# A gated order of first transfers and a respread mixer in an eight-core hybrid decoder step

## The reference

```
h = rmsnorm(x);  [u|v|p|q|gates] = h @ w_in          # 512|512|256|256|3*1024 columns
A: vh = layernorm(gelu(v)); a = gelu(u) * (tril(W_s[g]) @ vh + b_s[g])   per chunk of 128
B: mean over the trailing 2/4/8/16 rows of p, minus p, then a grouped linear layer
C: 4-head attention of q into 256 memory tokens
   prompt: k, v = rmsnorm(mem) @ w_kv;  sample: k, v are given per sequence
x += (sig(gA)*(a@Wa) + sig(gB)*(b@Wb) + sig(gC)*(c@Wc)) @ w_o
x += relu(rmsnorm(x) @ w_up)^2 @ w_down;  y = rmsnorm(x)
```

## Time and profile before

| | |
|---|---|
| median of 3 runs | 1034.17 us (1028.15 to 1060.0) |
| the profiled execution | 1025.52 us |
| its span, slowest core (core 1) | 1023.8 us |
| spans of all cores | 1016.1 to 1023.8 us |
| mean granted PE clock of core 1 | 0.969 |
| PE busy | 931.6 us (91%) |
| DVE, ACT, POOL busy | 384.8, 294.8, 274.1 us |
| first PE instruction | 35.85 us |

### The profile page before, as it was taken

One profiled execution on the slowest core, in us unless ns is written; L12 is line 12 of the kernel. 1 busy time (PEld: TensorE's weight loads), 2 busy tenths in 40 slices (PEclk: granted clock), 3 DMA queues, 4 the chain that ended last, 5 costly groups with the idle time before them and its releaser, 6 DMA issues.

```text
span 1023.8 us, 15629 instructions; the slowest of 8 cores (1016.1 to 1023.8 us)
## 1 busy us (share of the span) xinstructions
PE 931.6 (91%) x5312; PEld 481.7 (47%) x5312; DVE 384.8 (38%) x640; ACT 294.8 (29%) x528; POOL 274.1 (27%) x280
## 2 busy tenths in 40 slices
PE   0485878887999999999999999999999999999996
PEld 0253444444555555555555554455444554455442
DVE  0356455544223223223553124412343224421476
ACT  0144535252222222222555320033001320033332
POOL 1114113223433433434333320032101230023243
PEclk9987898897999999999999999999999999999998
DMA  9856630449102222221505022040404004040034
GB/s 143 214 151 143 125 118 1 83 82 239 28 16 41 42 42 42 42 42 65 162 1 104 1 44 41 11 72 1 83 1 83 1 11 72 1 83 2 21 152 178
DMA packets 17081, 71.26 MB, mean 70 GB/s; under 512 B 2141, under 2 KB 3164, under 8 KB 13164
## 3 DMA queue, kind: packets, MB, share of 16 engines
q0 software_dynamic: 5472, 35.65, 20.6%
q1 hardware_dynamic: 11532, 34.61, 10.3%
HBM read 95.80 MB, written 10.22 MB: 104 GB/s over the span
## 4 chain that ended last, share of the span: by engine, by line
PE 89%; DMA 4%; DVE 2%; issue 2%; POOL 1%; SPq 1%; ACT 1%; DVEq 0%; POOLq 0%; ACTq 0%
PE bank L338 87%; DMA X<-x 3%; PE bank L341 2%; SPq L153 1%; POOL X L347 1%; DMA cvo<-fA 1%; DVE X L356 1%; ACT fA L344 0%; ACT CR L344 0%; DVE fA L356 0%; POOL stats L347 0%; DVE hT L362 0%; DVEq L125 0%; DVE X L353 0%; ACT X L344 0%
## 5 line engine op out<-in xcount | busy, mean ns | idle before, releaser
L338 PE MATMUL bank<-hT,slot 128*128 128x436 bf16 (+3 forms) x2480 | 471.0, 350 | 0.0
L338 PEld LDWEIGHTS bank<-hT,slot 128*128 128x128 bf16 x2480 | 241.8, 99 | 218.0 <-issue 8.9
L338 PE MATMUL bank<-slot,CR 128*128 128x512 bf16 (+1 forms) x1376 | 298.5, 378 | 0.0
L344 ACT ACTIVATE fA<-bank 128x436 f32<-128x436 f32 (+3 forms) x223 | 120.2, 542 | 373.8 <-PE bank L338 359.8
L338 PEld LDWEIGHTS bank<-slot,CR 128*128 128x128 bf16 x1376 | 134.0, 98 | 157.0
L356 DVE SCALAR_TENSOR_TENSOR X<-bank,stats,X 128x512 f32<-128x512 f32 x136 | 102.1, 751 | 119.4 <-PE bank L338 119.4
L344 ACT ACTIVATE fW<-bank 128x436 f32<-128x436 f32 (+2 forms) x106 | 56.2, 533 | 174.7 <-PE bank L338 173.7
L347 POOL TENSOR_TENSOR CR<-fA 128x436 bf16<-128x436 f32 (+1 forms) x69 | 66.5, 964 | 108.7 <-ACT fA L344 104.3
L347 DVE TENSOR_TENSOR fA<-bank,fA 128x436 f32<-128x436 f32 (+1 forms) x77 | 43.1, 605 | 106.7 <-PE bank L338 106.6
L347 DVE TENSOR_TENSOR CR<-fA 128x436 bf16<-128x436 f32 (+1 forms) x51 | 31.2, 612 | 116.6 <-ACT fA L344 116.6
L347 POOL TENSOR_TENSOR stats<-stats,cstt 128x1 f32<-128x1 f32 (+3 forms) x30 | 35.5, 1185 | 139.5 <-DVE stats L353 115.5
(11 more groups left out here) (87 smaller groups left out, 496.0 us busy)
## 6 DMA issues: line engine op xcount, KB each, us to landing
slot<-wpk POOLq DMA_DIRECT2D x30, 1024.0 KB, 12.3
X<-x SPq DMA_DIRECT2D x34, 512.0 KB, 11.8
y<-hT SPq DMA_DIRECT2D x17, 512.0 KB, 2.7
CR<-ck POOLq DMA_DIRECT2D x4, 512.0 KB, 8.0
CR<-cv POOLq DMA_DIRECT2D x4, 512.0 KB, 11.0
gb<-gvec SPq DMA_DIRECT2D x3, 512.0 KB, 15.3
CR<-mem SPq DMA_DIRECT2D x2, 512.0 KB, 8.9
fW<-gbv SPq DMA_DIRECT2D x4, 256.0 KB, 14.0
```

The costliest lines, as they stand in the source:

```text
L338: s.op("pe", lambda e: e.matmul(out, lhsT=lhsT, rhs=rhs, start=start, stop=stop), R_, W_)
L344: s.op("act", lambda e: e.activation(out=out, in_=in_, func=func, **kw), R_, W_)
```

## The change

It does these things:

- **Transfers at the start.** `dma` and `load_next` take an `after` list of buffers whose last transfer is waited for. The load of v waits for x tile 0, pq for x tile 2, u for v, kv for pq. The window tables (`bnd`) are loaded ahead of the memory, and x tiles 4 to 6 ahead of the spatial-gate setup.
- **Block 0.** `P` and `WIN(0)` come ahead of the memory norms, squares of tiles 4 to 7 are laid between the gelus of `U`, `KV` comes ahead of `MIX`. `KV`'s evictions move from ACT to DVE, its bf16 copies from POOL to ACT.
- **Blocks 1 to 3.** The order inside a block becomes Q, V, S, P with `vout`, WIN, AV, U, MIX. Squares and multiplications of the next block's tiles are laid into a block ahead.
- **Sample tile.** Its norm, transpose and `Q(4)` stay in block 1, at its end. `V(16)`, `P(16)`, `WIN(4)`, and u and the gate (now `U4` and `MIX4`, one wide call each) go to block 3.
- **Sample attention.** `SA2` is cut in two (`SA2b` is its second half), and the steps are spread between P, WIN, AV and U.
- **Stores.** The `cvo` and `pool` outputs use tiles of the `xst` or `xnA` ring (`tS`) in place of `fA` and `fW`; the 16 small `pool_s` transfers are one. The first merge product (`WPO(0)`) is made ahead of the last `MIX`.

```diff
-    def dma(self, queue, pairs, reads=(), writes=(), owner=None):
+    def dma(self, queue, pairs, reads=(), writes=(), owner=None, after=()):
...
+        for b in self._flat(after):
+            op.deps.append(b.last_w)
...
-        load_next("v")
-        load_next("pq")
-        load_next("u")
+        x_b = [norm_src[t][1] for t in BT[0]]
+        load_next("v", after=[x_b[0]])
...
+            if i == 2:
+                load_next("pq", after=[x_b[2]])
...
+        load_next("u", after=[slot_b[0]])
+        s.dma("sp", [(bnd[:, B_CUR:B_SC], cb[:, B_CUR:B_SC])], writes=[bnd_b], owner=bnd_b)
         gm, gm_b = mem_loads()
-        load_next("kv")
+        load_x([4, 5, 6])
         setup_loads()
-        load_x([4, 5, 6])
...
         vfin()
+        load_next("kv", after=[slot_b[1]])
...
+        def tS(t):
+            if t == 16:
+                xn, xnb = ring("xn", xnA, xnA_b)
+                return xn.bitcast(F32), xnb
+            xt, xb = ring("xst", xst, xst_b)
+            return xt[:, 0:512], xb
...
-                    s.dma("sp", [(pool_s[b, 7:15, :], po[b * 8:(b + 1) * 8, 0:256]) for b in range(16)], reads=[po_b], owner=po_b)
+                    s.dma("sp", [(pool_s[:, 7:15, :], po[:, 0:256])], reads=[po_b], owner=po_b)
...
-                CP("act", f[:, 0:256], bk[:, 0:256], [bk_b], [f_b])
-                CP("pool", v_p[:, t, :], f[:, 0:256], [f_b], [vp_b])
+                CP("dve", f[:, 0:256], bk[:, 0:256], [bk_b], [f_b])
+                CP("act", v_p[:, t, :], f[:, 0:256], [f_b], [vp_b])
...
             S(j, 0)
             S(j, 1)
             if j >= 2:
-                SA1(2 * (j - 2))
-                SA1(2 * (j - 2) + 1)
...
+                SA1(g0)
+                SA1(g1)
+            for i in range(4):
+                P(BT[j][i])
+                vout(i)
+            if j == 3:
+                flush()
+                P(16)
+                vout(4)
...
+                    if g == 0:
+                        norm_sq(n16, 16)
+                        norm_b(*n16)
+                        N(16)
+                        load_x([12])
...
+                T(16)
+                Q(4)
...
+            if j == 3:
+                WPO(0)
...
+            if j == 3:
+                MIX4(*u4)
```

More of the change, by code:

```diff
@@ L387, in build_program, with load_next @@
         ld = {"n": 0}
-        def load_next(expect=None):
+        def load_next(expect=None, after=()):
             if ld["n"] >= len(order):
@@ L410, in build_program, with norm_new, norm_sq, norm_b @@
         xn_of = {}
-        def norm_a(ts):
[L413 to L423, removed]
+        def norm_new(n):
+            c = statcols(2 * n)
+            return [c, n, s.buf("st%d" % c), 0]
+        def norm_sq(nb, t):
+            c, n, sb_, i = nb
+            nb[3] += 1
+            xt, xb = norm_src[t]
+            xn, xnb = ring("xn", xnA, xnA_b)
+            ACT(xn, xt, AF.Square, [xb], [xnb, sb_], accum_out=stats[:, c + i:c + i + 1])
+            xn_of[t] = (xn, xnb, c + n + i, sb_)
+        def norm_a(ts):
+            nb = norm_new(len(ts))
+            for t in ts:
+                norm_sq(nb, t)
+            return nb
+        def norm_b(c, n, sb_, _):
             TS("dve", stats[:, c:c + n], stats[:, c:c + n], 1.0 / 1024, EPS, ALU.mult, ALU.add, [sb_], [sb_])
@@ new lines, in MIX, with U4 @@
+            tm, tm_b = tA()
+            STT(tm[:].rearrange("p (t i) -> p t i", i=128), bk[:, :].rearrange("p (t i) -> p t i", i=128), gvcol[:, g:g + 1],
+                CC[0][:, g:g + 1, :].broadcast_to([128, 4, 128]), ALU.mult, ALU.add, [bk_b, CC_b[0], cst_b], [tm_b])
+            TT("pool", apre[:, g, c0:c1], tm[:], ug[:], ALU.mult, [tm_b, ug_b], [apre_b[g][j]])
+        def U4():
+            w, wb = W("u", 8)
+            bk, bk_b = pb()
+            for g in range(4):
+                for k in range(8):
+                    MM(bk[:, g * 128:(g + 1) * 128], w[:, k, g * 128:(g + 1) * 128], hT[:, k, 2048:2176], k == 0, k == 7, [hT_b[16], wb], [bk_b])
+            ug, ug_b = tW()
+            ACT(ug[:], bk[:, :], AF.Gelu_apprx_tanh, [bk_b], [ug_b])
+            return ug, ug_b
@@ new lines, in MIX4 @@
+        def MIX4(ug, ug_b):
+            bk, bk_b = pb()
+            for g in range(4):
+                MM(bk[:, g * 128:(g + 1) * 128], vhs[:, g * 128:(g + 1) * 128], wsT[1][:, g, :], True, True, [vhs_b, wsT_b[1]], [bk_b])
+            tm, tm_b = tW()
+            for g in range(4):
+                STT(tm[:, g * 128:(g + 1) * 128], bk[:, g * 128:(g + 1) * 128], gvcol[:, g:g + 1], CC[1][:, g, :], ALU.mult, ALU.add,
+                    [bk_b, CC_b[1], cst_b], [tm_b])
+            TT("pool", apre[:, :, 2048:2176], tm[:].rearrange("p (g i) -> p g i", g=4), ug[:].rearrange("p (g i) -> p g i", g=4), ALU.mult,
+               [tm_b, ug_b], [apre_b[g][4] for g in range(4)])
```

201 lines of the change are left out of this document (108 added, 93 removed).

## The result

| | before | changed |
|---|---|---|
| first comparison, median of 4 runs each | 1034.3 us | 996.2 us (987.8 to 996.4) |
| ratio, 95% interval | | 0.9631 [0.9556, 0.9706] |
| second comparison, beside three of its variants | 1035.8 us, 11 runs | 986.7 us, 6 runs |
| ratio, 95% interval | | 0.9532 [0.95, 0.9563] |

The account below looks back on a forecast made before the run. Before 246 us PE stands waiting for x tiles and in the blocks, at a lowered clock; behind it PE is busy. Gains 20 + 5 + 20 = 45 us: 1025.5 - 45 = 980.5, plus 6.5 towards the median, 987 us (969 to 1009).

Parts of the forecast that it names:

- Start to the first V: From the start to the first `V` product: it comes at 27 us instead of 43, within 23 to 31.
- the slow end: Start: x tiles beside weight loads move at some 50 KB a microsecond, so tile 2 lands at 21 us; 20 taken.
- To the scores: First `V` to block 0's scores: they start at 70 us instead of 90, 20 us gained, bounds 14 and 26.
- the ends 64 and 71: Start of block 0's scores: 64 us at 150 KB a microsecond beside weight loads, 71 at some 50.
- The end of block 0: Scores to end of block 0: tile 16's transpose and 5.8 us wait leave; 5 us gained (3 to 6).
- Blocks 1 to 3: 104 to 246 us: 14 us net from waits and 6 from the clock, together 20 us gained (8 to 27).
- The sum of 24.7: Blocks 1 to 3 and first merge tile: PE waits of 11.0 + 6.2 + 2.7 + 2.3 + 2.5 us, expected to go.
- the chain that I had on ACT: Blocks 1 to 3: table load, eight exponentials, four evictions of `P` and a correction, 8 to 10 us, make `WIN` wait 6.
- The price of nothing for POOL behind the gains: Block 3: POOL's `cvo` multiplications wait for their gain, with merge loads queued behind; priced at nothing, up to 5 us if uncovered.
- Rival 1: The start stays bound by bytes: scores at 80 us, 10 us earlier instead of 20; 35 us gained, 997 us; chance 0.20.
- Rival 2: Waits of blocks 1 to 3 only change names, no clock returned: 5 us there, 30 in all, 1002 us; chance 0.10.
- Rival 4: Slower: a clock of 0.81 carries into the merge and behind, 180 us less 45, about 1165 us; chance 0.04.

Follow-up runs that it names:

- e6: Changed kernel with the gates undone: v, pq and u issued at once, kv at its old place, block 0's new order kept; 997.3 us, ratio 0.9628.
- e2: Changed kernel with the start and block 0 of the kernel before, blocks 1 to 3 as changed; 1006.7 us, ratio 0.9809.
- e8: Changed kernel with two of the four `V` products put ahead of `Q` in block 1; 984.6 us, ratio 0.9579.
- e9: Changed kernel with the sample attention's spreading undone: `SA2b` directly behind its `SA2`, both `SA3` together; 993.1 us, ratio 0.9654.
- e10: Changed kernel with the `cvo` rows multiplied in their `fA` tiles again and the store sent earlier; 988.3 us, ratio 0.9607.
- e3: Changed kernel with the four `P` products put ahead of `S` in blocks 1 to 3; 987.4 us, ratio 0.9627.
- e11: e8 with, besides, the last `V` product of each block (in block 3 the last two) behind the scores; 996.8 us, ratio 0.9701.

## Why the prediction was right, and where its steps were off

| term | forecast | measured (means of cores) |
|---|---|---|
| first `V` | 43 to 27 | 41.2 to 25.7 |
| gain at the scores | 20 (14 to 26) | 22.0 |
| to the end of block 0 | 5 (3 to 6) | 15.2 - 13.6 = 1.6 |
| blocks 1 to 3 and the first merge tile | 20 (8 to 27) | (131.2 - 117.6) + (786.5 - 781.3) = 18.8 |
| sum | 45 | 42.4 |

The last but one term is the length from block 1 to the merge and from there to the end.

**Start to the first V**: right in sum, by errors that cancel. Tile 0 landed at 7.8 us (1.96 + 5.8), not 5.5; the 3.2 us of the earlier trace rows are those of a tile alone, and here the gain and the next tiles of its own queue travel with it, which is the likely cause. So v came at 8.39 + 14.5 = 22.9, not 19 to 20. But the tiles went faster than the slow end: tile 2 landed at 15.5 us, not 20, and tile 1's transpose came at 19.2, not 23. What the forecast left out is tile 3. The transpose of tile 2 stands behind the statistics of tile 3, which landed at 23.1, and PE waits 5.8 us there; v had landed 3.9 us before the first `V`. The chain that ended last names that tile too:

```profile
4.12 18.93 DMA X<-x
```

On seven cores it is tile 3, on core 0 it is v, by 0.8 us. e6 shows that the gates cause the gain. The loads of pq, u and kv were issued 3.3 to 5.8 us behind the landing that they wait for, since a power that isn't ready stands in front of each in POOL's order; PE lost nothing by it, but for at most 1.4 us for pq on core 0.

**To the scores**: between the ends 64 and 71, at 65.8. No one waits for u or kv, as forecast. The gate tables were not "just ahead": the setup product waits 1.96 us for `wpb` on core 3 and up to 4.2 on others. Both ends came from a rate beside weight loads. The rule of "DMA: Bandwidth & Descriptors" in the Trainium skill, section "Queues, rings and completion order", would have given 71; the trace lies between it and the row of 150 KB a microsecond. While tile 3 travelled beside v, from 15.5 to 23 us, the two queues moved 0.81 and 0.79 MB, as by that rule.

**The end of block 0** is a step that failed: 1.6 us, not 5, below the range of 3 to 6. The wait of 5.8 us for tile 16 left, but I let nothing take its place. Two waits did (PE, 67 to 81 us):

```profile
PE bank L341 <- DVE hT L365: 2.5, 1, 2.5
PE bank L341 <- DVE fA L359: 2.2, 3, 1.5
```

The last copies into `hT`, which the transpose of tile 16 had covered, now stand directly ahead of `Q`, and `S` waits for banks that `MIX` still holds. e2 tells the two apart: with the old block 0, where `KV` lies between `MIX` and `S`, it has the 2.5 us for `hT` and none for `MIX`'s banks, and wins 3.8 us here. So the rest goes to the new block 0. e8 removes the wait for `hT`: 10.9 us instead of 13.6.

**Blocks 1 to 3**: right in sum, with the gain from waits too high and that from the clock too low, and with the wrong waits named, so in part by luck. The waits: 14 net forecast; idle time fell by 21.9 - 14.7 = 7.2, and by 2.6 in the first merge tile, 9.8. The sum of 24.7 that was to go held the 5.0 us around `S`, for which no step of mine takes the cause away; they have become the 5.6 for `ACT CR` and the 1.8 for `DVE CR`. Of the new waits, `WIN` was priced at 6 us (3.2, 1.5, 1.5) and has 1.8. Waits of 2.6, 1.5 and 1.5 us are there, but they belong to the product behind `S`, which needs a bank from the exponentials: the head of the chain that I had on ACT, another waiter, and sizes that agree by luck. Tile 16 costs 2.0 + 1.1 = 3.1 us for up to 3 (1.1 on three of the cores), `SA2b` 1.8 for 1. Not named were the 5.6, 1.9 for the norm of tile 8 and 0.6 for `S`'s last bank. The clock: 6 us forecast, 13.3 - 6.8 = 6.5 returned, and 2.0 in the first 25 us of the merge, from the windows there. That the spreading hides the `fW` copies is shown by e9, at 7.8 us. The wait for `cvo` left as forecast, but not for the reason given, since e10 has the rows in their old tiles and no such wait on PE. The price of nothing for POOL behind the gains holds: POOL stands 6.3 us for one, and PE is busy for 45.84 of the 45.84 us from the first merge product on.

**The rivals.** Rival 1 (bytes) fell: `V` is not behind 33, no wait for u or kv; the gates move the bytes that are needed first, and give back 5.7 of 16.2 (e6). Rival 2 is half true by its own mark: waits of 14.8 us are left in blocks 1 to 3, more than the 12 that I had set, those around `S` did change their names, and so do those of e3, e8 and e11. It fell in its price: 18.8 us were won here, not 5, since the other waits went and the clock came back. Rival 4 fell: 724 of 724 us at 1.00 behind 246, though one run of e9 did take 1167.5 us, with cores 0 to 3 at 0.81, which is its price. Where it says that the trace of the kernel before agrees for 57 to 60 us alone, 118 to 124 us stood at 0.81 too. "TensorE: Matmul & The Clock Gate" of the Trainium skill, section "Seeing it yourself", has 0.81 hold for a whole die while dense products last; the single runs of 1073 to 1168 us are like that, but in this profile the longest dense stretch is free of it, and in the first comparison's it held on two cores alone (core 1: 0.81 from 85 to 96 us) and was 1.00 there too from 246 to 986 us.

**The sum**: 42.4 by the spans, 1025.52 - 983.95 = 41.6 by the profiled executions, 3 less than the 45 forecast. The first median, 996, lies 9 above the forecast because three of its four runs have pairs; without them the runs are 984 to 988. That these meet 987 so closely owes something to the 6.5 us that I added, which stood for no step.

## What to carry to other kernels

Order the first transfers by need and hold back the rest with a wait on the landing: the same bytes brought the first product 16 us earlier, and 11 to 14 of them lasted. Where a step is moved away, ask which waits it had covered. When a wait has the forecast size, still look at which instruction stands in it: e11 was built on a wait that was read as `WIN`'s and was a wait for a bank. And move work between dependent steps by the queue of every engine that it touches: in e8 and e11, reorderings that looked free on PE lost what they won to statistics and evictions queued on DVE behind a transfer, or on ACT behind the exponentials.

## What was not expected of the hardware

Waits in the mixer can cost more than their length. In the table the time lost to the clock rises with the idle time on the whole (e3 lies above the others), from 14.7 and 6.8 us to 25.8 and 13.3, not against it. Windows of the changed kernel around two waits (columns as in the earlier trace rows) show how:

```profile
93.50:96.17 2.67, 0.10 (x1) 0.03 (x1) 0.91 (x4) 2.64 (x5) 1.52 (x2) 1.00 0.00 0
...
97.40:100.50 3.10, 3.10 (x18) 2.20 (x16) 0.67 (x2) 2.74 (x8) 1.47 (x3) 0.51 0.43 71
...
104.70:106.63 1.93, 0.08 (x2) 0.03 (x1) 1.93 (x3) 1.23 (x2) 0.00 (x0) 1.00 0.99 142
...
107.70:110.90 3.20, 3.20 (x18) 1.49 (x15) 3.20 (x4) 1.23 (x2) 0.00 (x0) 0.50 1.07 169
```

PE stands for 2.6 and 1.9 us, works for about 1 us, and then runs at 0.50, the lower level of 1.2 GHz, for 3.1 and 3.2 us, which loses another 1.5 and 1.6. Not every wait has such a tail: behind the 2.48 us that end at 81.15 the clock stays at 1.00. So by these three a wait is worth one to almost two times its length, and which of them is not seen in the waits themselves.
